# The first two weight tiles of each projection, fetched and split inside the projection ahead of it

## The chip, the cores and the metric

The kernel runs on one core of one Trainium2 chip. The metric is the device time of one execution of the whole program in microseconds (us); lower is better. The engines are TensorE (PE, matrix products), VectorE (DVE), ScalarE (ACT), GpSimd (POOL) and SyncE (SP), which here only issues DMAs. Each has its own instruction stream; they meet through semaphores.

## The reference

One encoder layer over 1024 tokens of width 1024 in float32, cut to the matrix products and the order in which they depend on each other:

```python
mod = silu(c) @ w_ada + b_ada                       # six vectors of 1024
h = rms_norm(x, g_pre_mix) * (1 + sc1) + sh1
p = h @ w_in                                        # 7 x 1024 columns
q, k, v, z, gates = split(p)
o = diff_attention(rope(q), rope(k), v, lam)        # 8 heads, two softmax maps each
y_attn = (rms_norm(o, g_subln) * 0.8).reshape(S, -1) @ w_attn_branch
sg = spatial_gating(gelu(z), gmlp_ln_g, gmlp_ln_b, w_spatial, b_spatial)
y_gmlp = sg @ w_gmlp_branch
mix = (sigmoid(gates_a) * y_attn + sigmoid(gates_g) * y_gmlp) @ w_out
x = x + gt1 * rms_norm(mix, g_post_mix)
h2 = rms_norm(x, g_pre_ffn) * (1 + sc2) + sh2
y = peer(h2, w_peer_q, peer_sub_keys, peer_u, peer_v)   # 8 heads, 16 of 128*128 experts each
x = x + gt2 * rms_norm(y, g_post_ffn)
```

## The kernel before

Activations lie with channels on the 128 partitions and tokens along the free dimension, as 8 chunks of 128x1024. Every large product takes three passes of TensorE: a matrix is split into a high part (float32r, a copy by ScalarE) and a low part (the rest, a subtraction by VectorE), and `product3` adds high x high, high x low and low x high.

The program is a row of stages. Each is one or more blocks; at the end of a block all five engines meet in a barrier, so the slowest of them sets when the next block begins. In order: `conditioning` (loads, rotary tables, the first 16 chunks of `mod`), the first norm, `attention`, the projection "front" (the gate half of z), the mean and `spatial` blocks, the projection "spat", `head_norm`, the projection "attn", the projection "out", `add_normed` and the second norm, the projection "rq" (queries of the expert lookup, with 16 tiles and the top-16 search), and then the routing and expert stages, which take about half of the program.

Five stages call `projection`. It runs over output tiles `j` of 128 channels (8, in "rq" 16). A weight tile is 512 KB: SyncE loads it into `raw[:, s]` with s = j mod 2 (`weights`), ScalarE copies it to `w_hi[:, s]`, VectorE writes `w_lo[:, s]` (`split` in both), TensorE multiplies (`tile`), and ScalarE and VectorE take the result out of PSUM (`empty`, with `own` given by the caller). All this is ordered by counting semaphores: `w_split` counts split tiles, `product` finished ones. In the steady loop the split of tile j+2 stands right behind the emptying of tile j. The first two tiles are loaded and split ahead of the loop, so TensorE's first matmul waits for a load, a copy and a subtraction.

Four of the projections ("front", "spat", "attn", "out") also carry a second stream: chunks of the expert matrix `peer_u` of 512 KB, 6, 4, 2 and 4 for each tile, that TensorE transposes between its matmuls. SyncE loads them (`row_chunks`), TensorE turns them (`turn_rows`), ScalarE copies them out and issues the store. For j = 0 TensorE meets the first of them behind k = 0 in "front", behind k = 1 in "spat" and "out" and behind k = 3 in "attn" (three matmuls for each k). SyncE issues its DMAs in program order: the first two weight tiles, what `sync_ahead` adds (two tables of "front", `c` in "out", the keys in "rq"), then in the loop `weights(2, 0)`, the row chunks of tile 0, `weights(3, 1)`, and so on, and `weights(j)` waits until tile j-2 is split. In "spat" and "attn" GpSimd loads a gate of 512 KB for each tile, in "out" two groups of `w_ada` of 1 MB each for each tile.

`attention` has weight buffers of its own, one raw tile and a ring of two split ones. Its last head (`LAST`, 8 blocks of 128 queries, b = 0 to 7) projects less than the others, so its later blocks have less to do.

Of the kernel before, what the change touches and what calls it, by code (L numbers as in the profile page):

```python
# [17 lines left out]
F32 = mybir.dt.float32  # L18
F32R = mybir.dt.float32r
# [7 lines left out]
P = 128  # L27
# [32 lines left out]
class Layer:  # L60
# [27 lines left out]
    def build(self):  # L88
        nc = self.nc
        with self.ctx:  # L90
# [55 lines left out]
            lists = [far.enter_context(nc.sbuf_tensor(name, [P, NG, P], dt, side="right"))  # L146
                     for name, dt in (("expert_at", U32), ("expert_of", U32), ("weight_of", F32))]
            lists.append(far.enter_context(nc.sbuf_tensor("dots", [P, 2, P], F32, side="right")))
            self.route(hi, lo, lists)
# [8 lines left out]
    def conditioning(self, x):  # L158
# [3 lines left out]
        NBUF = NOW // 2  # L162
# [12 lines left out]
        with ExitStack() as s:  # L175
# [12 lines left out]
            with nc.Block() as block:  # L188
                @block.sync
                def _(sp):  # L190
# [11 lines left out]
                    for g in range(NBUF):  # L202
                        sp.dma_start(ada[:, g], a["w_adaT"][:, 2 * g:2 * g + 2, :]).then_inc(ada_loaded[g], 16)
# [25 lines left out]
                def _(dve):  # L229
# [34 lines left out]
                    for j in range(NOW):  # L264
                        g = j // 2
                        dve.wait_ge(ada_loaded[g], 16)
# [4 lines left out]
                        dve.tensor_tensor_reduce(out=junk[:, j % 2], in0=ada[:, g, j % 2], in1=cb[:], scale=1.0,  # L271
# [138 lines left out]
    def projection(self, name, wt, first, x_hi, x_lo, tiles, act_out=None, dve_out=None, pe_after=None, dve_after=None, pool_program=None,  # L410
                   segments=None, rows=None, sync_ahead=None, act_ahead=None, dve_ahead=None, dve_before=None):
# [14 lines left out]
        with ExitStack() as c:  # L426
            raw = self.sb(c, f"{name}_w_raw", [P, 2, D])
            w_hi = self.sb(c, f"{name}_w_hi_t", [P, 2, KT, P], F32R)
            w_lo = self.sb(c, f"{name}_w_lo_t", [P, 2, KT, P], F32R)
# [15 lines left out]
            with nc.Block() as block:  # L445
                @block.sync
                def _(sp):
# [6 lines left out]

                    def row_chunks(j, s):
# [4 lines left out]
                    for s in range(2):  # L460
                        weights(s, s)
# [6 lines left out]
                    for s in range(2):  # L468
                        row_chunks(tiles - 2 + s, s)
# [5 lines left out]
                def _(act):  # L475
# [18 lines left out]
                    for s in range(2):  # L494
                        split(s, s)
# [7 lines left out]
                    for s in range(2):  # L503
                        empty(tiles - 2 + s, s, own)

                @block.vector
                def _(dve):
                    dve.sem_inc(w_split, 2)
# [11 lines left out]
                    for s in range(2):  # L520
                        split(s, s)
                    if dve_ahead:
                        dve_ahead(dve)
                    if dve_after is None:
# [5 lines left out]
                        for s in range(2):  # L530
                            empty(tiles - 2 + s, s, own)
                    else:
# [70 lines left out]
    def attention(self, h_hi, h_lo):  # L603
# [60 lines left out]
        def has(h, i):  # L664

            return i == VV or h < LAST
# [1991 lines left out]
```

## Time and profile before

| | |
|---|---|
| runs | 4437.38, 4446.63, 4445.62 us; median 4445.62 us |
| profiled execution, its own time | 4450.32 us |
| span of its instructions | 4448.6 us |
| mean granted TensorE clock | 0.906 of full speed |
| busy share of the span | PE 83%, VectorE 65%, ScalarE 34%, GpSimd 28% |

The profile is of one execution. Its span runs from the first instruction to the end of the last; its own time is 1.7 us longer. A busy share is a mean over stages with different limits; the stages that this case is about lie between 940 and 1770 us.

### The profile page before, as it was taken

The numbers are of one execution on the slowest core, as the hardware profiler recorded it, in microseconds if no ns is written. First come the engines' busy times: TensorE is split into PE (matmuls) and PEld (weight loads), VectorE is DVE, ScalarE is ACT, GpSimd is POOL, SyncE is SP. The second block draws the span as 40 slices with busy tenths as digits, with TensorE's granted clock in tenths as the row PEclk, the third lists the DMA queues.
The fourth block names the chain that finished last, engine by engine and source line by source line (L and its number), as shares of the span: only waits on it lengthen the run. The fifth ranks groups of instructions, "written<-read, shape, count | busy, mean of one in ns | idle before, by whom it ended". The sixth has DMA issues, their size and how long they took to land. (4 is left out here: it accounts for less than half of the span.)

```text
span 4448.6 us, 49413 instructions
## 1 busy us (share of the span) xinstructions
PE 3688.1 (83%) x17692; PEld 2798.9 (63%) x17692; DVE 2885.6 (65%) x5550; ACT 1526.3 (34%) x2208; POOL 1263.1 (28%) x1072
## 2 busy tenths in 40 slices
PE   5899999989597895987667535699999999999995
PEld 4677777768585674876556434466666666665553
DVE  5666666631613364887778768677677777776565
ACT  3444444435442443115666611122222212221211
POOL 0000000000100000000002236577666766675452
PEclk8999999989597996998888767899999999999997
DMA  3111111139193693102456688999999999999996
GB/s 140 43 48 50 50 53 53 48 131 392 52 342 120 240 410 121 38 15 95 133 161 195 206 276 302 350 401 406 378 399 401 402 379 394 405 402 369 359 373 241
DMA packets 384682, 1042.21 MB, mean 234 GB/s; under 512 B 33504, under 2 KB 102496, under 8 KB 381280
## 3 DMA queue, kind: packets, MB, share of 16 engines
q0 software_dynamic: 152352, 563.15, 33.3%
q1 hardware_dynamic: 179920, 334.33, 21.8%
q10 hardware_dynamic: 52208, 142.10, 8.3%
q8 instruction: 119, 1.95, 0.2%
q14 instruction: 83, 0.68, 0.0%
HBM read 897.37 MB, written 142.08 MB: 234 GB/s over the span
## 5 line engine op out<-in xcount | busy, mean ns | idle before, releaser
L2337 POOL DMA_INDIRECT ex_v_rows<-peer_v_dram,expert_of x512 | 629.1, 1229 | 293.7 <-PE psum L2566 147.3
L2469 DVE TENSOR_TENSOR y<-y,psum 128x512 f32<-128x512 f32 x512 | 349.3, 682 | 383.5 <-PE psum L407 380.9
L405 PE MATMUL psum<-h_hi 128*128 128x512 f32 x1024 | 422.2, 412 | 65.7 <-ACT sc_gelu_t L2086 52.7
L2329 POOL DMA_INDIRECT ex_u_rows<-u_rows_scratch,expert_at x352 | 394.6, 1121 | 269.2 <-DVE dots L2462 177.8
L2462 DVE CUSTOM_DVE_ANT_1 ex_u_rows<-ex_u_rows,y 128x1024 f32<-128x1024 f32 x352 | 429.4, 1220 | 58.3 <-DMA ex_u_rows<-u_rows_scratch,expert_at 42.6
L405 PE MATMUL psum<-h_hi,v_hi 128*128 128x512 f32 x1024 | 430.5, 420 | 1.1 <-DVE v_lo L2506 1.1
L406 PE MATMUL psum<-h_lo,h_hi 128*128 128x512 f32 x1024 | 408.3, 399 | 0.0
L407 PE MATMUL psum<-h_hi,h_lo 128*128 128x512 f32 x1024 | 406.9, 397 | 0.0
L406 PE MATMUL psum<-h_lo,v_hi 128*128 128x512 f32 x1024 | 405.4, 396 | 0.0
L407 PE MATMUL psum<-h_hi,v_lo 128*128 128x512 f32 x1024 | 404.4, 395 | 0.0
L2566 PE MATMUL psum<-ex_v_rows,ex_spread 128*32 128x512 f32 x2048 | 285.0, 630 | 98.4 <-DMA ex_v_rows<-peer_v_dram,expert_of 97.7
L1158 POOL TENSOR_TENSOR sp_sg<-sp_sg,sp_u 128x1024 f32<-128x1024 f32 x8 | 20.6, 2573 | 1191.2 <-DVE sp_sg L1218 1186.5
L405 PE MATMUL psum<-in_hi,att_w_hi_t 128*128 128x512 f32 x768 | 316.3, 412 | 36.8 <-DVE att_w_lo_t L859 35.0
L405 PEld LDWEIGHTS psum<-h_hi,v_hi 128*128 128x128 f32 x1024 | 194.9, 190 | 225.6 <-issue 126.7
L2187 PE MATMUL psum<-sc_first,sc_second 128*128 128x128 f32 x1024 | 178.3, 346 | 166.6 <-DVE sc_second L2014 166.5
L2380 ACT ACTIVATE h_hi<-g 128x512 fp32r<-128x512 f32 x128 | 80.8, 631 | 681.8 <-DVE g L2492 437.9
L407 PE MATMUL psum<-in_hi,att_w_lo_t 128*128 128x512 f32 x768 | 302.1, 393 | 0.0
L406 PE MATMUL psum<-in_lo,att_w_hi_t 128*128 128x512 f32 x768 | 301.5, 393 | 0.0
L405 PEld LDWEIGHTS psum<-h_hi 128*128 128x128 f32 x1024 | 199.1, 194 | 142.4 <-issue 91.9
L2187 PEld LDWEIGHTS psum<-sc_first,sc_second 128*128 128x128 f32 x1024 | 164.3, 252 | 197.5 <-DVE sc_second L2014 197.4
L407 PEld LDWEIGHTS psum<-h_hi,h_lo 128*128 128x128 f32 x1024 | 197.5, 193 | 43.5
L407 PEld LDWEIGHTS psum<-h_hi,v_lo 128*128 128x128 f32 x1024 | 195.2, 191 | 44.3
(380 smaller groups left out, 7912.1 us busy)
## 6 DMA issues: line engine op xcount, KB each, us to landing
y<-peer_v_dram SPq DMA_DIRECT2D x128, 512.0 KB, 8.4
route_scratch<-sc_stage SPq DMA_DIRECT2D x32, 1024.0 KB, 10.2
g<-route_scratch SPq DMA_DIRECT2D x128, 256.0 KB, 6.3
att_raw<-w_in_dram SPq DMA_DIRECT2D x48, 512.0 KB, 3.6
front_r_in<-peer_uT_dram SPq DMA_DIRECT2D x48, 512.0 KB, 6.6
u_rows_scratch<-front_r_out ACTq DMA_DIRECT2D x48, 512.0 KB, 6.7
sc_u_raw<-peer_uT_dram SPq DMA_DIRECT2D x48, 512.0 KB, 4.8
y<-peer_uT_dram ACTq DMA_DIRECT2D x40, 512.0 KB
```

The costliest lines, as they stand in the source:

```text
L405: pe.matmul(out, w_hi, x_hi, start=start, stop=False)
L406: pe.matmul(out, w_hi, x_lo, start=False, stop=False)
L407: return pe.matmul(out, w_lo, x_hi, start=False, stop=stop)
L1158: pool.tensor_tensor(sg[:, j % 2], sg[:, j % 2], u[:, j % 2], ALU.mult).then_inc(gated, 1)
L2187: last = pe.matmul(to, second[:, s, tok], first[:, s, tok], start=True, stop=True)
L2329: pool.indirect_dma_start(u_rows[:, r], None, every_u, bass.IndirectOffsetOnAxis(ap=expert_at[:, n // P, n % P:n % P + 1], axis=0)).then_i ...
L2337: pool.indirect_dma_start(v_rows[:, r * LANES + lane], None, every_v, bass.IndirectOffsetOnAxis(ap=expert_of[:, m // 32, t:t + 1], axis=0) ...
L2380: act.activation(act_hi[ring], g[:, s], ACT.Copy).then_inc(a_hi_done, 1)
L2462: dve.tensor_tensor_reduce(out=halves(u_rows[:, r]), in0=halves(u_rows[:, r]), in1=rows, scale=1.0, scalar=0.0, op0=ALU.mult, op1=ALU.add, ...
L2469: dve.tensor_tensor(to, to, ps[:, n % 4], ALU.add).then_inc(added, 1)
L2566: last = pe.matmul(ps[lane * 32:(lane + 1) * 32, 4 + half], spread[:, first:first + 32], v_rows[:, r * LANES + lane, half * HALF:(half + 1 ...
```

## The change

The split weight buffers `w_hi` and `w_lo` are allocated once, from the program's start to the end of the projection "rq", and all projections and `attention` use them. A projection gets an argument `following`, the weights of the next one. Behind its own last two tiles it loads and splits the first two tiles of those: SyncE has two more loads ahead of the row chunks of its last two tiles, ScalarE and VectorE one more `split` behind the emptying of each of the last two tiles. `attention` does the same for "front" in the blocks b = 6 and b = 7 of its last head. At the start of a projection the two loads and the splits are gone, and the semaphores begin at the values that they had behind them, which also lets `weights(2, 0)` go at once. The room for the buffers comes from `conditioning`, whose ring of `w_ada` groups has 6 slots for its 8 groups, and from four small lists that are allocated later. The loads and splits of "rq"'s tiles 2 to 15 and the instructions of TensorE stay as they were.

```diff
@@ build
+            weights = c.enter_context(ExitStack())
+            self.w_hi = self.sb_right(weights, "w_hi_t", [P, 2, KT, P], F32R)
+            self.w_lo = self.sb_right(weights, "w_lo_t", [P, 2, KT, P], F32R)
@@ conditioning
-        NBUF = NOW // 2
+        NBUF = 6
...
-                    for g in range(NBUF):
-                        sp.dma_start(ada[:, g], a["w_adaT"][:, 2 * g:2 * g + 2, :]).then_inc(ada_loaded[g], 16)
+                    for g in range(NOW // 2):
+                        if g >= NBUF:
+
+                            sp.wait_ge(mod_dot, 2 * (g - NBUF + 1))
+                        sp.dma_start(ada[:, g % NBUF], a["w_adaT"][:, 2 * g:2 * g + 2, :]).then_inc(ada_loaded[g % NBUF], 16)
@@ projection, SyncE
+                    def next_weights(s):
+                        sp.wait_ge(w_split, tiles + s + 1)
+                        sp.dma_start(raw[:, s], following[s]).then_inc(loaded[s], 16)
...
-                    for s in range(2):
-                        weights(s, s)
                     if sync_ahead:
                         sync_ahead(sp)
...
                     for s in range(2):
+                        if following:
+                            next_weights(s)
                         row_chunks(tiles - 2 + s, s)
@@ projection, ScalarE (VectorE has the same two edits)
-                    for s in range(2):
-                        split(s, s)
                     if act_ahead:
                         act_ahead(act)
...
                     for s in range(2):
                         empty(tiles - 2 + s, s, own)
+                        if following:
+                            split(tiles + s, s)
...
-                    dve.sem_inc(w_split, 2)
+                    dve.sem_inc(w_split, 4)
@@ projection, TensorE
                     pe.sem_inc(emptied, 2)
+                    pe.sem_inc(w_hi_done, 2)
+                    for s in range(2):
+                        pe.sem_inc(loaded[s], 16)
@@ attention, SyncE and ScalarE
+                    for s in range(2):
+                        load(NEXT + s, ZV0 + s)
...
+                            if h == LAST and b in NEXT_AT:
+                                s = NEXT_AT.index(b)
+
+                                act.wait_ge(out_summed, 8 * h + 6 + 2 * s)
+                                split_weights(NEXT + s)
@@ attention, VectorE
+                            if h == LAST and b in NEXT_AT:
+                                split_weights(NEXT + NEXT_AT.index(b))
```

What this does to SyncE's queue where "front" begins. Before, two weight tiles stand ahead of the tables; `front_r_in` is the first row chunk:

```order
L453 DMA front_w_raw<-w_in_dram 128x1024 x2
L1079 DMA sp_w<-w_spatial_dram 128x1024
L1080 DMA sp_bias<-b_spatial_dram 128x1024
L464 UNCONDITIONAL_BRANCH
L464 ISA
L453 ISA
L453 DMA front_w_raw<-w_in_dram 128x1024
L458 ISA
L459 ISA
L459 DMA front_r_in<-peer_uT_dram 128x1024
```

Now the tables come first, and the first row chunk is the fourth DMA of the block instead of the sixth:

```order
L1099 DMA sp_w<-w_spatial_dram 128x1024
L1100 DMA sp_bias<-b_spatial_dram 128x1024
L468 UNCONDITIONAL_BRANCH
L468 ISA
L455 ISA
L455 DMA front_w_raw<-w_in_dram 128x1024
L464 ISA
L465 ISA
L465 DMA front_r_in<-peer_uT_dram 128x1024
```

VectorE's rows at the end of "front", before the change. The last two instructions on `zv_total_t` empty tiles 6 and 7, and the block ends behind them:

```order
L1092 TENSOR_TENSOR zv_total_t<-zv_total_t,zv 128x1024
L512 TENSOR_TENSOR front_w_lo_t<-front_w_raw,front_w_hi_t 128x1024
L526 REGISTER_ALU
L526 COMPARE_AND_BRANCH
L1092 TENSOR_TENSOR zv_total_t<-zv_total_t,zv 128x1024 x2
L445 UNCONDITIONAL_BRANCH
```

The same place now: a split stands behind each of the two, the second of them as the last instruction of the block:

```order
L1112 TENSOR_TENSOR zv_total_t<-zv_total_t,zv 128x1024
L518 TENSOR_TENSOR w_lo_t<-front_w_raw,w_hi_t 128x1024
L530 REGISTER_ALU
L530 COMPARE_AND_BRANCH
L1112 TENSOR_TENSOR zv_total_t<-zv_total_t,zv 128x1024
L518 TENSOR_TENSOR w_lo_t<-front_w_raw,w_hi_t 128x1024
L1112 TENSOR_TENSOR zv_total_t<-zv_total_t,zv 128x1024
L518 TENSOR_TENSOR w_lo_t<-front_w_raw,w_hi_t 128x1024
L447 UNCONDITIONAL_BRANCH
```

The splits moved from behind the block's opening barrier to just ahead of its closing one; "spat", "attn" and "out" have the same two shapes.

## Rows read from the trace of the kernel before

**Rows 1.** The head of the page.

```profile
span 4448.6 us, 49413 instructions
```

**Rows 2.** Timeline, start of "front": start us, length us, engine, line, what, [idle before <-releaser]. "q" is a sequencer.

```profile
965.56 0.80 SPq L453 DMA_DIRECT2D front_w_raw<-w_in_dram  x2
...
969.23 1.06 ACT L480 ACTIVATE front_w_hi_t<-front_w_raw 128x1024 fp32r<-128x1024 f32 x1 [7.15 <-DMA front_w_raw<-w_in_dram]
970.32 1.23 DVE L512 TENSOR_TENSOR front_w_lo_t<-front_w_raw,front_w_hi_t 128x1024 fp32r<-128x1024 f32 x1 [16.25 <-ACT front_w_hi_t L480]
971.68 0.79 PE L405 MATMUL psum<-in_hi,front_w_hi_t 128*128 128x512 f32 x1 [10.23 <-DVE front_w_lo_t L512]
972.35 11.54 SPq L459 DMA_DIRECT2D front_r_in<-peer_uT_dram  x6
...
977.03 1.96 PE L580 MATMUL psum<-ident,front_r_in 128*128 128x128 f32 x8 [3.70 <-DMA front_r_in<-peer_uT_dram]
```

**Rows 3.** The tile sp_bias: its only load, issued at 966.9 us.

```profile
DMA to landing us min/median/max: 7.5/7.5/7.5
```

**Rows 4.** Timeline, start of "spat".

```profile
1216.06 6.89 SPq L453 DMA_DIRECT2D spat_w_raw<-w_gmlp_dram  x3
1223.24 2.54 SPq L459 DMA_DIRECT2D spat_r_in<-peer_uT_dram  x4
...
1227.72 1.97 PE L580 MATMUL psum<-ident,spat_r_in 128*128 128x128 f32 x8 [2.23 <-DMA spat_r_in<-peer_uT_dram]
```

**Rows 5.** Timeline, start of "attn".

```profile
1413.82 6.42 SPq L453 DMA_DIRECT2D attn_w_raw<-w_attn_dram  x3
...
1419.86 0.79 PE L405 MATMUL psum<-in_hi,attn_w_hi_t 128*128 128x512 f32 x1 [12.65 <-DVE attn_w_lo_t L512]
1425.40 1.24 PE L580 MATMUL psum<-ident,attn_r_in 128*128 128x128 f32 x8
```

**Rows 6.** Timeline, start of "out".

```profile
1532.42 0.80 SPq L453 DMA_DIRECT2D out_w_raw<-w_out_dram  x2
...
1539.12 0.53 POOL L1475 DMA_DIRECT2D out_ada<-w_adaT_dram  x1 [21.99 <-DVEq L1445]
...
1539.15 2.21 SPq L459 DMA_DIRECT2D out_r_in<-peer_uT_dram  x4
...
1543.62 1.09 PE L580 MATMUL psum<-ident,out_r_in 128*128 128x128 f32 x8 [2.20 <-DMA out_r_in<-peer_uT_dram]
1547.39 2.29 DVE L1460 TENSOR_TENSOR out_products<-out_ada,out_cb 128x2048 f32<-128x2048 f32 x1 [6.70 <-DMA out_ada<-w_adaT_dram]
...
1565.38 1.71 PE L580 MATMUL psum<-ident,out_r_in 128*128 128x128 f32 x8 [4.83 <-DMA out_r_in<-peer_uT_dram]
```

**Rows 7.** Timeline, start of "rq".

```profile
1752.15 0.81 SPq L453 DMA_DIRECT2D rq_w_raw<-w_peer_dram  x2
...
1758.17 0.79 PE L405 MATMUL psum<-h_hi,rq_w_hi_t 128*128 128x512 f32 x1 [30.69 <-DVE rq_w_lo_t L512]
1761.50 2.29 DVE L1629 TENSOR_TENSOR k_lo<-k_raw,k_hi 128x2048 fp32r<-128x2048 f32 x1 [2.12 <-ACT k_hi L1623]
```

**Rows 8.** Timeline, the ends of "front" and of "out".

```profile
1110.38 1.22 DVE L1092 TENSOR_TENSOR zv_total_t<-zv_total_t,zv 128x1024 f32<-128x1024 f32 x1 [15.05 <-ACT zv L1086]
...
1112.03 3.50 PE L1102 MATMUL psum<-zv_total_t,ones_mean 128*128 128x512 f32 x4 [2.85 <-PEq L445]
...
1675.47 1.02 ACT L1453 ACTIVATE mixed<-psum 128x1024 f32<-128x1024 f32 x1
...
1675.66 1.22 DVE L1467 TENSOR_TENSOR out_total<-out_total,out_sq 128x1024 f32<-128x1024 f32 x1 [4.06 <-ACT out_sq L1452]
```

**Rows 9.** Timeline, block b = 7 of attention's last head.

```profile
948.73 1.28 DVE L907 SCALAR_TENSOR_TENSOR att_map<-att_prob,att_zr 128x1024 f32<-128x1024 f32 x1
...
950.58 1.03 PE L1006 MATMUL psum<-ident,att_map 128*128 128x128 f32 x8
```

**Rows 10.** Timeline, conditioning: the 11th of 16 dots on w_ada.

```profile
35.62 1.23 DVE L271 CUSTOM_DVE_ANT_0 junk<-ada,cb 128x1024 f32<-128x1024 f32 x1 [1.13 <-DMA ada<-w_adaT_dram]
```

More of the change, by code:

```diff
@@ L145, in build @@
                 self.stage_end()
[L146 to L149, printed above, removed]
+            lists = self.route(hi, lo, far, weights)
             y = far.enter_context(nc.sbuf_tensor("y", [P, KT, T], F32, side="right"))
@@ L270, in _ @@
                             dve.wait_ge(lam_dots, 2)
-                        dve.tensor_tensor_reduce(out=junk[:, j % 2], in0=ada[:, g, j % 2], in1=cb[:], scale=1.0,
+                        dve.tensor_tensor_reduce(out=junk[:, j % 2], in0=ada[:, g % NBUF, j % 2], in1=cb[:], scale=1.0,
                                                  scalar=0.0, op0=ALU.mult, op1=ALU.add,
@@ L410, in projection @@
     def projection(self, name, wt, first, x_hi, x_lo, tiles, act_out=None, dve_out=None, pe_after=None, dve_after=None, pool_program=None,
-                   segments=None, rows=None, sync_ahead=None, act_ahead=None, dve_ahead=None, dve_before=None):
+                   segments=None, rows=None, sync_ahead=None, act_ahead=None, dve_ahead=None, dve_before=None, following=None):
         nc = self.nc
@@ L519, in empty @@
                             own(dve, j, s, acc[s], emptied)
-                    for s in range(2):
-                        split(s, s)
                     if dve_ahead:
@@ L531, in _ @@
                             empty(tiles - 2 + s, s, own)
+                            if following:
+                                split(tiles + s, s)
                     else:
@@ L662, in side_weights @@
             return 2 + 6 * h + (2 * f + 1 if h < LAST else f + 1)
+        NEXT = side_weights(LAST, 2) + 1
+        NEXT_AT = (6, 7)
         def has(h, i):
@@ L1092, in dve_out @@
                 dve.tensor_tensor(total[:], total[:], zv[:, bass.ds(j, 1)].rearrange("p o t -> p (o t)"), ALU.add).then_inc(summed, 1)
-            self.projection("front", a["w_in"], ZV0, h_hi, h_lo, KT, act_out=act_out, dve_out=dve_out, rows=ROWS_FRONT,
+            self.projection("front", a["w_in"], ZV0, h_hi, h_lo, KT, act_out=act_out, dve_out=dve_out, rows=ROWS_FRONT, following=a["w_gmlp"],
                             sync_ahead=load_tables, dve_ahead=clear_total)
@@ L1380, in dve_out @@
                 dve.tensor_tensor(column(wide, j), acc, gate[:], ALU.mult).then_inc(emptied, 1)
-            self.projection("spat", self.a["w_gmlp"], 0, x_hi, x_lo, KT, act_out=act_out, dve_out=dve_out, rows=ROWS_SPAT,
+            self.projection("spat", self.a["w_gmlp"], 0, x_hi, x_lo, KT, act_out=act_out, dve_out=dve_out, rows=ROWS_SPAT, following=self.a["w_attn"],
                             pool_program=self.load_gates(gate, KT, None, 2, g_loaded))
@@ L1410, in dve_out @@
                 dve.tensor_tensor(column(m_lo, j), column(wide, j), column(m_hi, j).bitcast(F32), ALU.subtract).then_inc(m_split, 1)
-            self.projection("attn", self.a["w_attn"], 0, x_hi, x_lo, KT, act_out=act_out, dve_out=dve_out, rows=ROWS_ATTN,
+            self.projection("attn", self.a["w_attn"], 0, x_hi, x_lo, KT, act_out=act_out, dve_out=dve_out, rows=ROWS_ATTN, following=self.a["w_out"],
                             dve_ahead=nothing_added, pool_program=self.load_gates(gate, 0, added, 1, g_loaded))
@@ L1475, in pool_program @@
                         pool.dma_start(ada[:, s], a["w_adaT"][:, bass.ds(at[s], 2), :]).then_inc(ada_loaded[s], 16)
-            self.projection("out", a["w_out"], 0, m_hi, m_lo, KT, act_out=act_out, dve_out=dve_out, rows=ROWS_OUT, pool_program=pool_program,
+            self.projection("out", a["w_out"], 0, m_hi, m_lo, KT, act_out=act_out, dve_out=dve_out, rows=ROWS_OUT, following=a["w_peer"], pool_program=pool_program,
                             sync_ahead=load_c, act_ahead=bend_c, dve_ahead=clear_total, dve_before=ada_groups)
@@ L1553, in finish, with route @@
                             self.a["out"].rearrange("(k p) t -> p k t", p=P))
-    def route(self, h2_hi, h2_lo, lists):
+    def route(self, h2_hi, h2_lo, far, weights):
         with ExitStack() as c:
@@ L1561, in route @@
             self.stage_end()
+            weights.close()
+            lists = [self.sb_right(far, name, [P, NG, P], dt) for name, dt in (("expert_at", U32), ("expert_of", U32), ("weight_of", F32))]
+            lists.append(self.sb_right(far, "dots", [P, 2, P]))
             self.token_rows(h2_hi, h2_lo)
```

9 lines of the change are left out of this document (4 added, 5 removed).

## The prediction

> **What bounds the kernel now.** I read the page first, for the span [rows 1] and for the fact that the program is a chain of stages with a barrier behind each. So what counts is not a busy share but how long TensorE stands still at each of the five places where a projection begins. Then I read the timeline around each of them, engine by engine, and looked for two things: what released TensorE's first matmul, and what stopped it next.
>
> In "front" SyncE issues the first load at 965.56, ScalarE's copy begins at 969.23, VectorE's subtraction at 970.32, TensorE at 971.68 [rows 2]: 6.1 us of load, copy and subtraction with nothing beside them. But TensorE then does three matmuls and stands again, 3.70 us, until 977.03, because the first row chunk has not landed. That chunk was issued only at 972.35: it stands in SyncE's queue behind the load of tile 2, which waits for the split of tile 0. "spat" repeats this, with a second stop that ends at 1227.72 [rows 4], and so does "out", until 1543.62 [rows 6]. In "attn" twelve matmuls come before the first chunk, and it is there in time [rows 5]. "rq" has no row chunks: only its start at 1758.17 waits [rows 7]. So in three of five projections the quantity to forecast is not when TensorE starts but when the first row chunk lands.
>
> **The starts.** In all five TensorE can now begin about 0.3 us behind the opening barrier, which is at SyncE's first issue of before.
>
> *rq.* SyncE's first issue is at 1752.15, the first matmul at 1758.17 [rows 7]. The start moves to about 1752.4: a gain of 5.8. The keys (1 MB) were split at 1763.8 (1761.50 plus 2.29). TensorE needs them behind its tile 0 and tile 1; they now stand first in the queue and come some 2 us sooner, while TensorE needs them 5.8 sooner, and a tile is over 10 us long. Hidden. The top-16 search is fed by TensorE and moves with it. 5.8, between 5.3 and 6.1.
>
> *attn.* Start 1419.86 to about 1414.1, 5.8 sooner. TensorE then comes to the first chunk after 5.5 us (1425.40 less 1419.86), at 1419.6. The chunk is issued behind one load. Before, the third load of the row went out at 1419.9 (1413.82 plus 6.42, less its own issue time), and the chunk was there at 1425.40 at the latest, 5.5 us on; 5.5 us behind 1413.82 is 1419.3 [rows 5]. In time. I take 5.8; if the chunk were 1.7 late (below), 4.1.
>
> *spat.* The third load went out at 1222.6 (1216.06 plus 6.89, less its issue) and TensorE resumed at 1227.72, 5.1 us later [rows 4]. The same pair now goes out from 1216.06: 1221.2. GpSimd's gate load now runs beside it. Its price: in "front" the first load took 3.7 us (969.23 less 965.56) and the fourth landed at 974.4 (966.9 plus 7.5), so three more cost 5.2 us, 1.7 each [rows 2, 3]; sharing with the gate costs half of one, 0.8. 1222.0, a gain of 5.7, between 4.5 and 6.5.
>
> *front.* The chunk is now the fourth DMA of the block, behind sp_w, sp_bias and the load of tile 2. The fourth DMA of before landed 8.8 us behind the first issue (974.4 less 965.56) [rows 2, 3]. So it lands at about 974.4 instead of 977.0, and TensorE, having started at 965.9, stands from 967.5 to there. 2.6, between 0.5 and 4.5. The start itself moves by 6 us, and more than half of that turns into a longer second wait.
>
> *out.* The chunk was issued at 1539.15 and used at 1543.62, 4.5 us later, with one weight load and the first group of `w_ada` ahead of it [rows 6]. Now `c` (512 KB) stands ahead of both in SyncE's queue, and GpSimd, which waited for a VectorE semaphore that stood behind the splits, issues both groups (2 MB) at about 1533.0 and 1533.7, ahead of the chunk at 1533.8. `c` has a head start and costs about 1, the second group, sharing, about 1: 1533.8 + 4.5 + 2 = 1540.3, a gain of 3.3. Later TensorE stands 4.83 us at 1565.38 for a row chunk: there the stage is bound by bytes, and the stream of bytes starts 6.1 us sooner with one more transfer of 1.7 in it, 4.4. Between 3.3 and 4.4 I take 4.0; bounds 1.1 and 6.1.
>
> At the same place a rule can be weighed. The row shows that the chunk, issued 0.03 us behind GpSimd's first group, was used at 1543.62, and the group at 1547.39: the small transfer did not wait for the large one [rows 6]. The Trainium skill (DMA: Bandwidth & Descriptors, Queues, rings and completion order) states that a completion lands only after every earlier write of that DMA engine, across its queues. By that rule the chunk would have to stand behind both groups in full, and the gain in "out" would be about 1.1. The trace of before speaks against the strict form, for one group.
>
> Sum of the starts: 2.6 + 5.7 + 5.8 + 4.0 + 5.8 = 23.9.
>
> **The ends.** The two added loads for each projection go out in time: they stand ahead of the row chunks of the last two tiles and wait for a split made a tile and more before. The split behind tile 6 lies where every tile has one and TensorE works on tile 7. The split behind tile 7 has no cover. "front" ends with VectorE's addition, 1110.38 to 1111.6, and the next block's matmul follows at 1112.03 [rows 8]: the barrier waits for VectorE. ScalarE's copy of 1.06 fits beside that addition, VectorE's subtraction of 1.23 comes behind it: 1.2 us later. "spat" and "attn" end with a VectorE instruction of the same size and get the same 1.2. In "out" ScalarE is late too: its last copy ends at 1676.5, the weight copy at 1677.5, the subtraction at 1678.7, where VectorE had ended at 1676.9: 1.8. In `attention` the split at b = 6 stands ahead of VectorE's chain for b = 7: the map ended at 950.0, will end at 951.2, and TensorE was ready for it at 950.58: 0.6 [rows 9]. The split at b = 7 lies beside TensorE's last product. Last, "out" takes 1 MB more while its DMAs are full; its last stop for a chunk is long past by then, and I charge 0.3, bounds 0 and 2.6. Sum: 3 x 1.2 + 1.8 + 0.6 + 0.3 = 6.3.
>
> **conditioning.** Groups 6 and 7 now wait for dots 2 and 4. The 11th dot had to wait 1.13 us for group 5 [rows 10]; the six dots between dot 4 and it took 1.2 us each, so dot 4 was done some 8 us earlier, while group 5 was still in the queue. The loads stay gapless: 0. If the queue had run dry there, each group would cost two of those 1.7, some 3.5.
>
> **Net.** 23.9 - 6.3 = 17.6. The profiled execution took 4450.3 (1.7 more than its span); the median of the runs shown is 4445.6, 4.7 lower. Taken from the median: 4428.
>
> **The rivals.**
> - *The first row chunk is late in "out"* (behind all of GpSimd's groups), with "spat" at its lower bound: 2.9 and 1.2 less, saving 13.5, 4432. For it: 2 MB are issued ahead of the chunk; against it: the row above. Chance 0.15.
> - *The second wait takes it all.* The row chunks land when they landed before, so that "front", "spat" and "out" gain nothing: 11.6 - 6.3 = 5.3, 4440, within what can be told. For it: that wait already exists in three places. Against it: the chunk is issued 5 to 6 us sooner in each. It decides when chunks need 9 us and more after a lone load; the longest there was 5.1. Chance 0.12.
> - *The tails are free* (another engine holds the barriers anyway): 3 to 5 us more, 4423. Against it: the matmul at 1112.03 comes 0.4 behind VectorE's end. Chance 0.07.
> - *Slower: a prefetched tile comes late.* In "out" SyncE's second added load queues in a full stage; a split that waits for it holds the barrier, and each us costs one. In that stage a tile's data would have to come after 1676; the load goes out about 25 us before. The kernel is slower by more than 0.2% only if tiles come some 50 us after issue, and the longest chunk wait of TensorE there is 4.83 [rows 6]. 4455; chance 0.02.
>
> **How the numbers follow.** The forecast as worked out has 0.64. What a measurement of this kernel can tell from no change is about 0.2%, 8.9 us. Faster: 0.64 + 0.15 + 0.07 = 0.86; same 0.12; slower 0.02. The bounds of the terms give a saving between 8 and 23, and the runs of before lie within 9 us of each other; with the rivals, 4418 to 4440 holds eight in ten.
>
> **What the profile will show.** First matmuls of projections within 0.5 us of the barrier; in "front" and "spat" a wait for the first row chunk of 5 to 7 us and of some 3 us, longer than before; in "attn" none or under 1. VectorE's `w_lo_t` as the last instruction of four blocks, and the distance from tile 7's last matmul to the next block longer by 1.2, in "out" by 1.8. "rq" from first matmul to the end unchanged. The forecast is wrong if the waits for the first chunk end as far behind the barrier as before, or if "out" shows new stops at its tiles 6 and 7.

## The result, and the profile after

The changed kernel takes 4461.96 us (median of 7 runs, 4454.83 to 4467.53), the kernel before 4446.63 in its runs beside it (4437.38 to 4453.63). The ratio is 1.0031, 95% interval 1.0021 to 1.0042 (an estimate of its own from the single runs; the two medians alone give 1.0034): slower by 0.3%, where 0.4% faster was forecast. The profiled execution took 4467.5, its span is this:

```profile
span 4465.8 us, 49428 instructions
...
PE 3714.4 (83%) x17692; PEld 2801.5 (63%) x17692; DVE 2882.2 (65%) x5550; ACT 1524.5 (34%) x2208; POOL 1264.2 (28%) x1072
```

That is 17.2 us over [rows 1]. I first compared when TensorE reaches the same instruction in both traces. At the last matmul of `attention` the changed kernel is 22.2 us late (983.24, against 961.06), though only two splits were added there. Behind it the lag shrinks: at the first row turn of "front" 19.1, of "spat" 17.1, of "attn" 16.4, of "out" 18.2, at the first score of "rq" 12.3; then it grows to 16.3 by the end of "rq". So the starts did gain, and the loss lies where no instruction was moved.

The groups of the products with the projection weights, on the page of the profile, show what is longer. First the kernel before (`attention` alone), then the changed kernel, where `attention`, "front", "spat" and "attn" share the names (out<-in, partitions x elements, xcount | busy us, mean ns | idle before):

```profile
L405 PE MATMUL psum<-in_hi,att_w_hi_t 128*128 128x512 f32 x768 | 316.3, 412 | 36.8 <-DVE att_w_lo_t L859 35.0
...
L407 PE MATMUL psum<-in_hi,att_w_lo_t 128*128 128x512 f32 x768 | 302.1, 393 | 0.0
L406 PE MATMUL psum<-in_lo,att_w_hi_t 128*128 128x512 f32 x768 | 301.5, 393 | 0.0
```

```profile
L408 PE MATMUL psum<-in_hi,w_hi_t 128*128 128x512 f32 x1152 | 486.8, 423 | 61.6 <-DVE w_lo_t L877 35.0
...
L409 PE MATMUL psum<-in_lo,w_hi_t 128*128 128x512 f32 x1152 | 463.2, 402 | 0.0
L410 PE MATMUL psum<-in_hi,w_lo_t 128*128 128x512 f32 x1152 | 462.3, 401 | 0.0
```

A mean of one overlaps its neighbours; what sets the time is the distance from start to start. TensorE's timeline in the middle of `attention`, before and after; from the first start to the second are eight distances in each fence:

```profile
299.64 0.39 PE L407 MATMUL psum<-in_hi,att_w_lo_t 128*128 128x512 f32 x1
...
301.46 0.39 PE L406 MATMUL psum<-in_lo,att_w_hi_t 128*128 128x512 f32 x1
```

```profile
299.71 0.40 PE L410 MATMUL psum<-in_hi,w_lo_t 128*128 128x512 f32 x1
...
301.59 0.40 PE L409 MATMUL psum<-in_lo,w_hi_t 128*128 128x512 f32 x1
```

1.82 us against 1.88, 227 ns against 235. Over all of `attention` (130 to 940 us, some 2,000 distances) the median is 227 for each of the three products before, and 234 after. In the expert stages, whose operands are other tiles, it is 227 or 228 in both. `attention` has 3 x 768 such matmuls; 7 ns for each make 16.1 us. The rest of its loss lies at the boundaries of heads. TensorE stands there for `att_q_lo` in both kernels, 2.0 us before and 1.9 after; before, the granted clock mostly stays 1.00, and after, it falls. Windows at one such boundary (from:to, length, PE busy, PEclk, DMA share, GB/s), first of the kernel before, then of the changed one:

```profile
326.00:330.00 4.00, 2.39 (x10) 1.00 0.18 66
330.00:335.00 5.00, 5.00 (x23) 1.00 0.00 0
```

```profile
326.00:330.00 4.00, 3.04 (x18) 1.00 0.00 0
330.00:332.00 2.00, 1.08 (x4) 0.94 0.35 131
332.00:335.00 3.00, 3.00 (x8) 0.50 0.00 0
```

For 3 us the clock is at its lower level (1.2 GHz), seven matmuls follow at 427 ns, and that costs 1.4. Before, this happens at one head boundary of `attention` (221 us) and three times in the last head; after, at six boundaries (332, 441, 550, 659, 769, 878) and again three times in the last head.

What had changed for these matmuls is only where their weights lie. The build gives each tile a byte address, the same on every partition. Before, all weight tiles start at multiples of 128 (`att_w_hi_t` at 97152, for one); the shared ones, allocated from the right-hand end, start 96 bytes past one (221152 and 212960). The activations `in_hi` and `in_lo` stand on multiples of 128 in both (18816 and 51584).

The starts, in the changed kernel's timeline. "front", then "spat", "attn", "out" and "rq":

```profile
987.67 0.33 SPq L1099 DMA_DIRECT2D sp_w<-w_spatial_dram  x1
...
989.48 2.08 SPq L465 DMA_DIRECT2D front_r_in<-peer_uT_dram  x4
989.82 0.79 PE L408 MATMUL psum<-in_hi,w_hi_t 128*128 128x512 f32 x1 [6.19 <-issue]
...
996.10 1.75 PE L589 MATMUL psum<-ident,front_r_in 128*128 128x128 f32 x7 [4.65 <-DMA front_r_in<-peer_uT_dram]
...
1236.98 0.35 SPq L455 DMA_DIRECT2D spat_w_raw<-w_gmlp_dram  x1
1237.75 3.49 SPq L465 DMA_DIRECT2D spat_r_in<-peer_uT_dram  x4
...
1238.86 0.79 PE L408 MATMUL psum<-in_hi,w_hi_t 128*128 128x512 f32 x1 [10.42 <-issue]
...
1244.81 1.54 PE L589 MATMUL psum<-ident,spat_r_in 128*128 128x128 f32 x6 [3.03 <-DMA spat_r_in<-peer_uT_dram]
...
1434.87 0.35 SPq L455 DMA_DIRECT2D attn_w_raw<-w_attn_dram  x1
...
1436.30 0.79 PE L408 MATMUL psum<-in_hi,w_hi_t 128*128 128x512 f32 x1 [8.26 <-issue]
...
1441.82 1.09 PE L589 MATMUL psum<-ident,attn_r_in 128*128 128x128 f32 x8 [0.29 <-DMA attn_r_in<-peer_uT_dram]
...
1551.63 0.33 SPq L1457 DMA_DIRECT2D out_cb<-c_dram  x1
...
1552.51 0.53 POOL L1495 DMA_DIRECT2D out_ada<-w_adaT_dram  x1 [17.51 <-DVEq L1465]
1552.94 2.21 SPq L465 DMA_DIRECT2D out_r_in<-peer_uT_dram  x4
...
1553.70 0.79 PE L408 MATMUL psum<-m_hi,w_hi_t 128*128 128x512 f32 x1 [10.59 <-issue]
...
1561.82 1.97 PE L589 MATMUL psum<-ident,out_r_in 128*128 128x128 f32 x8 [5.20 <-DMA out_r_in<-peer_uT_dram]
...
1768.82 0.33 SPq L1643 DMA_DIRECT2D k_raw<-keysT_dram  x1
...
1769.77 0.76 PE L408 MATMUL psum<-h_hi,w_hi_t 128*128 128x512 f32 x1 [25.54 <-PEq L559]
```

These answer to [rows 2] and [rows 4 to 7]: the load, copy and subtraction are gone in all five, and the second waits are 4.65, 3.03, 0.29 and 5.20 us. But TensorE starts 1 to 2.2 us behind SyncE, waiting for no semaphore that the rows show. The end of "front", beside [rows 8]:

```profile
1130.70 1.23 DVE L1112 TENSOR_TENSOR zv_total_t<-zv_total_t,zv 128x1024 f32<-128x1024 f32 x1 [14.10 <-ACT zv L1106]
1131.85 1.22 DVE L518 TENSOR_TENSOR w_lo_t<-front_w_raw,w_hi_t 128x1024 fp32r<-128x1024 f32 x1
1133.39 1.54 PE L1122 MATMUL psum<-zv_total_t,ones_mean 128*128 128x512 f32 x2 [3.87 <-PEq L447]
```

### The profile page after: what moved, and what is told of

Same layout as the page of the kernel before. It is cut to its first block and busy times, and to the rows that moved or that the text cites. A ratio compares the mean times of both kernels' runs of the same rounds, so it can differ in the third digit from the quotient of the medians.

```text
span 4465.8 us, 49428 instructions
## 1 busy us (share of the span) xinstructions
PE 3714.4 (83%) x17692; PEld 2801.5 (63%) x17692; DVE 2882.2 (65%) x5550; ACT 1524.5 (34%) x2208; POOL 1264.2 (28%) x1072
## 5 line engine op out<-in xcount | busy, mean ns | idle before, releaser
L408 PE MATMUL psum<-in_hi,w_hi_t 128*128 128x512 f32 x1152 | 486.8, 423 | 61.6 <-DVE w_lo_t L877 35.0
L409 PE MATMUL psum<-in_lo,w_hi_t 128*128 128x512 f32 x1152 | 463.2, 402 | 0.0
L410 PE MATMUL psum<-in_hi,w_lo_t 128*128 128x512 f32 x1152 | 462.3, 401 | 0.0
L408 PEld LDWEIGHTS psum<-in_hi,w_hi_t 128*128 128x128 f32 x1152 | 222.3, 193 | 118.2 <-DVE w_lo_t L877 37.7
L410 PEld LDWEIGHTS psum<-in_hi,w_lo_t 128*128 128x128 f32 x1152 | 221.4, 192 | 53.8
```

The costliest lines, as they stand in the source:

```text
L408: pe.matmul(out, w_hi, x_hi, start=start, stop=False)
L409: pe.matmul(out, w_hi, x_lo, start=False, stop=False)
L410: return pe.matmul(out, w_lo, x_hi, start=False, stop=stop)
```

## The experiments

The theory going in: the weight tiles' place within 128 bytes slows the matmuls. The rivals: the far end of the memory, or the sharing of one pair of buffers; and the added loads and splits.

### The weight tiles moved by less than 128 bytes

In the changed kernel (a1; in a2 the pad has 8 words, in a3 16; a second pad ahead of `mixed` makes 128 bytes in all, so that nothing else moves by anything but 128):

```diff
+            self.pad = self.sb_right(weights, "pad_ahead", [P, 24])
             self.w_hi = self.sb_right(weights, "w_hi_t", [P, 2, KT, P], F32R)
...
-            lam2 = self.sb(s, "lam2", [P, 4])
+            lam2 = self.pad[:, 0:4]
```

In the kernel before (b1; `attention` likewise; b2 has the pads around `w_lo` alone, b3 around `w_hi`):

```diff
+            self.sb(c, f"{name}_pad_ahead", [P, 24])
             w_hi = self.sb(c, f"{name}_w_hi_t", [P, 2, KT, P], F32R)
             w_lo = self.sb(c, f"{name}_w_lo_t", [P, 2, KT, P], F32R)
+            self.sb(c, f"{name}_pad_behind", [P, 8])
```

> The changed kernel with 96 bytes of padding (which also take two small tiles of the conditioning) ahead of the shared weight tiles: their byte address on each partition goes from 96 past a multiple of 128 to a multiple of 128, as in the kernel before; nothing else moves by other than 128 bytes. Theory (the place of the stationary operand within 128 bytes slows every matmul that reads it): a matmul of 512 columns follows the one ahead of it after 227 ns instead of 234; attention's end stands within 2 us of where it stood before instead of 22 later; the projections lose nothing in their steady part; total about 4434 (4462 less 20 in attention, 1 in front, 2 in spat, 4 in rq and some tenths). Rival 1 (a far region of SBUF, or sharing one pair of buffers, costs it): 234 ns stays, 4462. Rival 2 (the added loads and splits in attention disturb it): 4462 too.

> The same with 32 bytes of padding: the tiles start 64 bytes past a multiple of 128. If what counts is a grid of 64 bytes: 227 ns and about 4434. If it is a grid of 128: 234 ns and about 4462. By the rivals 4462.

> The same with 64 bytes of padding: the tiles start 32 bytes past a multiple of 128, off both grids, and the two small tiles are moved too, so it shows whether the padding by itself does anything. By either grid: 234 ns, 4462. If padding of any size helps: 4434.

> The kernel before, with the order and the buffers of its own as they are, only that its weight tiles (attention's and each projection's) start 96 bytes past a multiple of 128; what lies behind them is padded back. Theory: 234 ns instead of 227, attention about 20 us longer, total about 4446 plus 27 = 4473, slower than the change that it doesn't have. Rivals (region, sharing, added loads): 4446.

> The kernel before with only the low half of its weight tiles 96 bytes past a multiple of 128, the high half on one. If the place counts for the stationary operand that a matmul itself reads: only the products with the low half follow at 234 ns (its group's mean 401 instead of 393 ns), the two with the high half stay at 227; a third of what the shift of both cost (29 us): 4446 plus 9 to 10, 4455. If it is something between the matmuls (the load of the next weights beside the running product): all three or a different one of them change. If it is the pair's distance from each other: another pattern, or 4475.

> The kernel before with only the high half of the weight tiles 96 bytes past a multiple of 128. With only the low half off, all three products of a triple slowed, from 227 to 231 to 233 ns, and the kernel took 15 us and more extra instead of 10. If what counts is that the two halves stand differently: the same again, 231 to 233 for all three, about 4462 to 4468. If every load of an off tile adds its share: two of three are off now, more than before, 233 to 234 and 4468 to 4475.

Measured, with the distances in `attention` (medians in ns, from the start of `w_hi` x `in_hi`, `w_hi` x `in_lo` and `w_lo` x `in_hi` to the next start; offsets are bytes past a multiple of 128; each ratio is to runs of the kernel before made beside that kernel, whose medians lie between 4444.02 and 4448.77):

| kernel | w_hi, w_lo, in | distances | median us | ratio to before, interval |
|---|---|---|---|---|
| before | 0, 0, 0 | 227, 227, 227 | | 1 |
| changed | 96, 96, 0 | 234, 234, 234 | 4461.96 | 1.0031 (1.0021 to 1.0042) |
| a1_aligned | 0, 0, 0 | 227, 227, 227 | 4436.30 | 0.9983 (0.9969 to 0.9996) |
| a2_at_64 | 64, 64, 0 | 234, 233, 233 | 4458.69 | 1.0031 (1.0017 to 1.0044) |
| a3_at_32 | 32, 32, 0 | 233, 232, 233 | 4453.84 | 1.0019 (1.0007 to 1.0031) |
| b1_before_off | 96, 96, 0 | 234, 234, 234 | 4475.59 | 1.0073 (1.0056 to 1.0090) |
| b2_low_off | 0, 96, 0 | 233, 232, 232 | 4467.93 | 1.0051 (1.0034 to 1.0067) |
| b3_high_off | 96, 0, 0 | 230, 232, 231 | 4465.33 | 1.0034 (1.0024 to 1.0044) |

The timelines of b1 and a1 at the place shown above, again eight matmuls from start to start (1.86 and 1.81 us; `attention`'s last matmul stands at 960.87 in a1):

```profile
299.67 0.39 PE L407 MATMUL psum<-in_hi,att_w_lo_t 128*128 128x512 f32 x1
...
301.53 0.40 PE L406 MATMUL psum<-in_lo,att_w_hi_t 128*128 128x512 f32 x1
```

```profile
299.83 0.39 PE L410 MATMUL psum<-in_lo,w_hi_t 128*128 128x512 f32 x1
...
301.64 0.39 PE L1016 MATMUL psum<-att_k_both,att_q_twice 128*128 128x512 f32 x1
```

With the same 96 bytes put right in the one kernel and wrong in the other, both follow: 26 us come back, 29 to 32 are lost. Region, sharing and added loads are out as the cause of it. A pad by itself doesn't bring the pace back (233 ns in a2 and a3), though a3 is 8 us quicker than the changed kernel, against 4462 expected. And one expectation on the mechanism missed. With only the low half off, I expected the one product that reads it to slow and 4455; all three slowed, to 4468. So a matmul isn't slow for its own operand alone. In b1 the distances of `att_k_both` x `att_q_twice`, whose operands both moved by 128 bytes and so stand as before, go from 227 to 231 ns too, and with `att_q_lo` to 235; in the changed kernel they are 233 and 231, while those of `att_a_hi_t` x `att_v_hi` stay at 227. With only the high half off (b3) all three slowed as well, and 4465 lies in the 4462 to 4468 expected if the two halves' standing apart is what counts; a sum of shares, 4468 and more, doesn't fit.

### All the operands moved together

h1 puts `self.sb(c, "pad_all", [P, 8])` ahead of all activations of the kernel before, h2 puts its weight tiles back. i1 does it to the changed kernel with 24 words, its weights where the change put them. f1 and c1 move the whole right-hand side by 96 bytes, onto multiples of 128, in the kernel before and in the changed one: in "out" that moves `m_hi` and `m_lo`, the activations there, in c1 the shared weights too.

> The kernel before with 32 bytes of padding ahead of all activations and weights: everything on the left-hand side, both operands of every product up to 'out' and in 'rq' and the expert stages, stands 32 bytes past a multiple of 128. If the place on the grid itself counts: 233 ns or more in all stages, in the expert stages' products too, and 30 to 60 us more, 4480 to 4500. If only the place of the operands to one another counts: 227 ns stays and 4446.

> The same with the weight tiles of attention and the projections put back on multiples of 128, so that in those products only the moving operand is 32 bytes off. In 'out' of the kernel before, where the moving operand alone was off, the three followed at 233, 235 and 232 ns. If the grid counts for each operand: 232 to 235 ns in attention too, and at or under the time of the kernel with both off. If the place to one another counts: 232 to 235 too, but slower than with both off by 20 us.

> The changed kernel with its shared weight tiles exactly where the change put them, 96 bytes past a multiple of 128, and 96 bytes of padding ahead of everything on the left-hand side, so that the activations stand 96 past too. If the place to one another counts: 227 ns in attention and the projections, attention's end within 2 us of the kernel before, total 4434 to 4437, as with the weight tiles moved to the activations. If the place on the grid counts: 234 ns or more and 4462.

> The kernel before with the whole right-hand side of the memory moved down by 96 bytes, onto multiples of 128: the moving operands of 'out' (m_hi, m_lo), and mixed, x1, the lists and y with it. Weight tiles stay where they were, on multiples of 128. If the moving operand counts too: 'out' follows at 227 instead of 232 to 235 ns, 384 matmuls by 6 ns, 2 to 2.5 us, and the rest the same: 4443 to 4444. If only the stationary one counts: 4446 and 'out' as before.

> The changed kernel with the same: its whole right-hand side, shared weight tiles and all, on multiples of 128. 'out' at 227 ns by the one theory, 232 to 235 by the other; total 4433 to 4434, against 4436 with the weight tiles alone moved.

| kernel | w_hi, w_lo, in | distances in `attention` | median us | ratio to before, interval |
|---|---|---|---|---|
| h1_all_at_32 | 32, 32, 32 | 227, 227, 227 | 4434.39 | 0.9961 (0.9946 to 0.9975) |
| h2_moving_off | 0, 0, 32 | 234, 234, 234 | 4462.31 | 1.0035 (1.0024 to 1.0046) |
| i1_left_at_96 | 96, 96, 96 | 227, 227, 227 | 4441.45 | 0.9989 (0.9980 to 0.9998) |
| f1_before_aligned | 0, 0, 0 | 227, 227, 227 | 4448.97 | 1.0007 (0.9997 to 1.0017) |
| c1_all_aligned | 0, 0, 0 | 227, 227, 227 | 4438.24 | 0.9979 (0.9968 to 0.9989) |

My theory of an absolute grid fell with h1: 32 bytes off, and the fast pace. i1 is the proof on the changed kernel itself: the weights stand at the same bytes, only the left-hand side with the activations moved, and it runs at 227. Again eight matmuls, 1.81 us:

```profile
299.68 0.39 PE L410 MATMUL psum<-in_lo,w_hi_t 128*128 128x512 f32 x1
...
301.49 0.39 PE L409 MATMUL psum<-in_hi,w_hi_t 128*128 128x512 f32 x1
```

So in `attention` what counts is how the weights stand to the rest of the left-hand side, in which `in_hi` and `in_lo` lie; no run moved these two alone, so that they are the partner is argued. How far apart is alike enough isn't settled either. In every kernel at 227 the weights and activations in fact stand a multiple of 512 bytes apart (97152 less 18816 is 153 x 512, 221056 less 18816 is 395 x 512), and in those at 230 ns and more at least one half of the weights stands 32, 64 or 96 bytes beyond such a multiple; 128 and 256 bytes beyond, for both halves, were not tried.

In "spat", "attn" and "rq" the same kernels have the longer distances as in `attention`. "out" does not bear the rule out as cleanly. The mean of its distances under 260 ns is 234.9 ns in the kernel before and 232.6 in a1, where the weights are at 0 and `m_hi` and `m_lo` at 96, and 229.1 in f1 and in c1, with all at 0. But it is 229.8 in h1, where the weights are at 32 and `m_hi` and `m_lo` still at 96. The gain of some 2 us that I expected of f1 and c1 can't be seen in the totals. The totals of c1 and i1 came out 4 to 5 us above those expected. (h1's 4434 is no sign of a faster pace: up to the end of "rq" it is within 1.7 us of the kernel before; see the section on the hardware.)

### The starts

d1 is a1 with the first row chunk of a projection first in SyncE's queue; g1 is the same on c1. j0 and j1 leave out half of each `w_ada` group in "out" (in the kernel before and in a1), j2 the same half in d1; VectorE multiplies the one chunk twice, so the vectors made there are not the reference's. These three ran once each.

```diff
+                    if rows:
+                        row_chunks(0, 0, range(1))
                     if sync_ahead:
                         sync_ahead(sp)
+                    if rows:
+                        weights(2, 0)
+                        row_chunks(0, 0, range(1, per_tile))
...
-                        pool.dma_start(ada[:, s], a["w_adaT"][:, bass.ds(at[s], 2), :]).then_inc(ada_loaded[s], 16)
+                        pool.dma_start(ada[:, s, 0:1], a["w_adaT"][:, bass.ds(at[s], 1), :]).then_inc(ada_loaded[s], 16)
```

> The changed kernel with its weight tiles on multiples of 128 (4436), and SyncE issues the first row chunk of a projection ahead of everything else in the block, ahead of the tables, of c and of the load of tile 2. If TensorE's second wait at a start is set by the chunk's place in the queue: the chunk lands 3.7 to 4.5 us behind the opening instead of 8.4, 7.1 and 10; 'front' gains 4.0, 'spat' 2.7, 'out' 5.5 at its first row turn and 1 to 3 at its end, 'attn' and 'rq' nothing; total 4427 to 4429. If a chunk waits for the bytes of all transfers that are issued about then, whichever queue they are in (GpSimd's two groups of 1 MB in 'out'): the first turn in 'out' stays 10 us behind the opening, and the total is 4429 to 4430.

> The changed kernel with the whole right-hand side on multiples of 128 and the first row chunk of each projection first in SyncE's queue. Sum of what the two did: 4429 to 4430 from the chunk, 0 to 2 less from 'out' at 227 ns: 4428 to 4430, 17 us (0.4%) under the kernel before. If the chunk's gain had come from elsewhere, 4436.

> The kernel before with half of each w_ada group left out in out (GpSimd loads one of its two chunks, VectorE multiplies that one twice; the vectors made there are not the reference's). If out is bound by its bytes: its eight tiles, from the first row turn to the last, take 8 us less or more than the 130.5 they took. If TensorE bounds it: no less.

> The same half left out in the changed kernel with its weight tiles on multiples of 128, where out gave back all but 2 us of what it gained at its start. Bound by bytes: with fewer bytes the gain at the start (from the opening to the last matmul, beside the kernel before with the same half left out) is 4 to 6 us. If something else takes it back: 2 us as now.

> The changed kernel with weight tiles on multiples of 128, half of each w_ada group left out in out, and the first row chunk first in SyncE's queue. If the late first chunk is what takes the gain at the start when the bytes are few: from the end of attn to the block behind out it is 5 to 6 us shorter than with the chunk late (j1), the gain of the first turn kept to the end. If the bytes still bound the stage, or something else: 0 to 2.

d1 took 4429.74 us (4427 to 4429 expected), ratio 0.9966 (0.9954 to 0.9978); g1 4425.86, 0.9951 (0.9937 to 0.9964). Times of TensorE in us, each from the last matmul of the work ahead (so they hold the end of that block too), first to the first row turn (in "rq" to the first score), then to the stage's last matmul:

| | before | changed | a1 | d1 | j0 | j1 | j2 |
|---|---|---|---|---|---|---|---|
| front, first turn | 15.97 | 12.86 | 12.63 | 9.25 | | | |
| front, last | 147.72 | 145.88 | 144.90 | 143.59 | | | |
| spat, first turn | 20.39 | 16.79 | 16.51 | 14.00 | | | |
| spat, last | 136.61 | 135.34 | 132.69 | 129.97 | | | |
| attn, first turn | 18.78 | 14.37 | 14.58 | 14.12 | | | |
| attn, last | 117.95 | 115.27 | 113.96 | 113.17 | | | |
| out, first turn | 19.05 | 19.10 | 20.24 | 13.70 | 20.08 | 19.70 | 13.69 |
| out, last | 149.46 | 146.19 | 147.49 | 147.80 | 137.64 | 137.82 | 134.84 |
| rq, first score | 56.22 | 51.80 | 50.39 | 50.13 | | | |
| rq, last | 246.68 | 246.27 | 240.85 | 240.58 | | | |

The chunk's place in the queue does set the second wait: in d1 the first turns of "front", "spat" and "out" come 3.4, 2.5 and 6.5 us sooner than in a1. In "out" of a1, the first turn:

```profile
1526.52 0.53 POOL L1497 DMA_DIRECT2D out_ada<-w_adaT_dram  x1 [17.23 <-DVEq L1467]
1526.95 2.42 SPq L466 DMA_DIRECT2D out_r_in<-peer_uT_dram  x4
...
1536.97 1.96 PE L590 MATMUL psum<-ident,out_r_in 128*128 128x128 f32 x8 [6.34 <-DMA out_r_in<-peer_uT_dram]
```

In d1, the first turn and the second:

```profile
1523.02 0.53 POOL L1504 DMA_DIRECT2D out_ada<-w_adaT_dram  x1 [17.23 <-DVEq L1474]
1523.06 0.33 SPq L466 DMA_DIRECT2D out_r_in<-peer_uT_dram  x1
...
1526.93 1.91 PE L597 MATMUL psum<-ident,out_r_in 128*128 128x128 f32 x8
...
1536.29 1.33 PE L597 MATMUL psum<-ident,out_r_in 128*128 128x128 f32 x8 [3.98 <-DMA out_r_in<-peer_uT_dram]
```

10.0 us from issue to use, against at most 3.9. In d1 the chunk, issued 0.04 us behind a group of 1 MB, was used 3.9 us later, and the group landed 7.4 us behind its issue. The Trainium skill (DMA: Bandwidth & Descriptors, Queues, rings and completion order) states that a completion lands only behind every earlier write of that DMA engine, across its queues. The prediction read "earlier write" as everything issued earlier, and d1 contradicts that reading; against writes that the engine has already done, which is what the sentence speaks of, these traces show nothing. What a1 has ahead of the chunk and d1 has not is `c`, a weight tile and 0.4 us of GpSimd's group; which of them holds it up wasn't tried.

Of the 6.5 us nothing is left at the end of "out" (147.49 and 147.80), and 3.0 of 6.0 with half of GpSimd's bytes left out (137.82 and 134.84). j0 against the kernel before shows why: 11.8 us less from leaving bytes out alone. "out" is bound by its bytes, and an earlier start of TensorE is given back. The rows show where. TensorE's waits for row chunks in "out" (those over 0.4 us) add up to 11.9 us in the kernel before, 12.0 in a1 and 12.4 in d1: d1 has none at the first turn, but 3.98 at the second and 2.78 and 3.02 later. With half of GpSimd's bytes only one such wait is left in each kernel. It is 3.3 us in j0 and 5.8 in j1, both at the first turn, so what j1 gained at its start went into the longer wait and it is no quicker than j0; and 2.7 in j2, at the second turn. I expected a gain of 4 to 6 in j1, and in j2 5 to 6 on j1; both missed.

### Two versions that are faster

i2 is the change with row chunks first and both sides 32 bytes off. k1 is g1 with one line:

```diff
+            self.sb(c, "sc_pad", [P, 8])
             key_of = self.sb(c, "sc_key_of", [SEL, KEYS])
```

> The changed kernel with the first row chunk first in SyncE's queue, and both sides of the memory 32 bytes past a multiple of 128 (32 bytes of padding on the left, 64 on the right). If the place to one another counts: 227 ns, in out too, and no more than the same kernel on multiples of 128, 4426. The kernel before with its left side at 32 also lost 15 us less in the routing stage (2020 to 2780 us), by something not yet named; if that comes from the place of the left side alone, 4411; if from its distance to the right side, which is the same here as in the kernel on multiples of 128, 4426.

> The changed kernel with all operands on multiples of 128 and the row chunk first (4426), and 32 bytes of padding ahead of sc_key_of in the routing stage: sc_second, sc_first, sc_stage, sc_u_raw and sc_rows_first move from 96 past a multiple of 128 to multiples of 128, and nothing else moves. If their place gave the two kernels their 12 to 18 us: the stage from 2070 to 2780 us is that much shorter, 4410 to 4415. If it was the distance to the tiles that stayed, or another tile: 4426.

i2 took 4415.35, ratio 0.9928 (0.9914 to 0.9941), 4 us above the lower of the two figures. k1 took 4406.10, ratio 0.9915 (0.9901 to 0.9929), 40 us (0.9%) under the kernel before, under the 4410 to 4415 expected. Beside g1, in the profiled runs, k1 is 2.7 us late when the routing stage begins and 21.6 early at 2750 us.

## Why the prediction was wrong, step by step

- **What TensorE does in between.** This is the step that failed. The prediction took TensorE's instructions as they were, charged `attention` 0.6 us, and had no term for the pace of a matmul; I never asked where the new buffers lie. Against a1 the changed kernel loses 22.4 us in `attention` (some 16 from the pace; and 111 matmuls of `attention` follow at some 427 ns where a1 has 77, by 0.2 each 6.8), 1.0 in "front", 2.7 in "spat", 1.3 in "attn" and 5.4 in "rq", and is 1.3 quicker in "out": 31.5, where the two spans differ by 31.4 (4465.8 and 4434.4). b1 shows the same without the change. No rival had it either: the one that was to be slower, a tile that comes late, did not happen. Of the prediction's own signs one points at it: "rq" from its first matmul to its last was to stay as it was, and took 219.7 us instead of 214.9 (214.5 in a1).
- **The change by itself.** With its weights standing as before (a1) it saves 7.7 us by the medians (4444.02 for the kernel before in that comparison; 0.17%, interval 0.04 to 0.31%) and 14.2 by the profiled spans, where 17.6 was forecast; the profiled execution of the kernel before, 4450.32, is over its median, and the stages below are read from it. The forecast 4428 misses a1's 4436 by 8.
- **The starts, 23.9 forecast.** By the table's last matmuls, before less a1: 2.8, 3.9, 4.0, 2.0 and 5.8, in all 18.5, with the longer end of "attn" (1.1) already taken off "out"'s. "front" (2.6) and "rq" (5.8) came out as forecast. In "spat" (5.7) the chunk was used 7.5 us behind the block's first issue in a1 (7.8 in the changed kernel) instead of 5.9. In "attn" (5.8) the mis-sized term is the start of TensorE: "0.3 us behind the opening barrier" measured, in the order of the five starts, 2.15, 1.88, 1.43, 2.07 and 0.95, so 1.1 too much was expected here; the rest of the 1.8 wasn't traced. That "rq" has its 5.8 in spite of 0.95 instead of 0.3 is luck in part. In "out" (4.0) the first turn did not come sooner at all (11.3 us behind the block's first issue in a1, 11.2 before), and the last matmul came 2.0 sooner, 3.0 without the end of "attn": its reading as bound by bytes was right, its first-chunk estimate (3.3) wrong. Of the rivals the late first chunk in "out" came nearest there; it gave 1.1.
- **The ends, 6.3 forecast.** From the last matmul to the first of the next block, a1 less before: "front" 4.29 less 3.25, 1.0; "spat" 8.67 less 7.52, 1.2; "out" 5.82 less 4.08, 1.7; "attn", to SyncE's first issue, 8.91 less 7.85, 1.1. The terms were 1.2, 1.2, 1.8 and 1.2. VectorE's `w_lo_t` closes the blocks, as foretold. The split at b = 6, given 0.6, can't be told from the rest in a1, whose `attention` ends 0.2 sooner.
- **conditioning, 0 forecast.** All sixteen dots start within 0.1 us of where they did.

## What the runs showed of the hardware

- In `attention` 128x512 matmuls followed each other at 227 ns from start to start where weights and activations stood a multiple of 512 bytes apart (before, a1, h1, i1, f1, c1), and at 230 to 234 where they stood 32, 64 or 96 bytes off that; the pace then also fell for some products whose own operands stood to each other as before. Which access causes it is open. So is why "out" of the changed kernel, with weights and `m_hi`, `m_lo` all at 96, has a mean distance of 230.4 ns, and of 228.4 in i1, where its other tiles were at 96 too.
- With the slower pace the granted clock fell to half for 3 us at six head boundaries instead of one, behind a stand of the same 2 us (the changed kernel, and b1 at the same six; a1 at none). Why is open.
- In the routing stage a move of `sc_second`, `sc_first`, `sc_stage`, `sc_u_raw` and their neighbours from 96 past a multiple of 128 to a multiple of it was worth about 24 us in the profiled runs. No instruction got shorter by more than a few ns (`sc_stage` copies 1078 and 1073); between 2040 and 2560 us the median load of `sc_u_raw` landed after 5.7 us instead of 6.9. Which of the tiles does it, and through what, wasn't tried. It fits h1, h2 and i2, where they stood at 0 too: from the first to the last product of `sc_first` the stage took 482 to 487 us in these three and k1, and 494 to 502 in the sixteen other kernels.

## What to carry to other kernels

A change that only reallocates a buffer changes its address: list the byte addresses of TensorE's operands before and after, and keep the distances between them as they were, or try them; here multiples of 512 were fast and 32, 64 or 96 bytes more were not. If a trace shows a loss where nothing was moved, compare the distance from start to start of the same matmuls before looking for waits. And in a stage bound by its bytes, order the transfers by who waits first, but count no gain until the stage's last instruction.
